# A two-block transformer kernel on one core: convolution taps moved between softmax steps, and VectorE's order at two other places

## The chip, the cores and the metric

One core of a Trainium2 chip. The metric is the device time of one launch in microseconds. Three runs of the kernel before took 1996.96, 1998.6 and 1999.41 us (median 1998.6). The profile shows one more execution of 1994.3 us.

## The reference, cut to what matters

512 tokens of width 1024, fp32, batch 1, two blocks one after the other. Only the parts that the change touches are spelled out.

```python
# first block
x = x + 0.5 * swiglu(rmsnorm(x), ffn1_wgu, ffn1_wdown)
z = rmsnorm(x) @ w_in               # q, k, v | ca, cb | ga, gb
a = sliding_window_attention(q, k, v, sinks) @ attn_proj     # window 128, 16 heads, 2 kv heads
u = ca * sigmoid(cb)
u = causal_depthwise_conv(u, dw_w, dw_b)                     # 31 taps, 1024 channels
c = silu(layernorm(u)) @ conv_proj
x = x + (sigmoid(ga) * a + sigmoid(gb) * c) @ w_out
x = x + 0.5 * swiglu(rmsnorm(x), ffn2_wgu, ffn2_wdown)       # the second FFN
e = rmsnorm(p @ ple_proj)
x = x + sigmoid(rmsnorm(x) @ ple_gate_w) * e
# second block
proj = rmsnorm(x) @ w_in_2          # pool | q, k, v | z | b, a
q, k, v = silu(causal_dwconv(q, k, v, 4 taps))
L = strict_lower(k_beta k^T * decay)                         # chunks of 64, 4 heads
T = inverse(eye + L)                                         # built level by level
# gated delta rule, w_out_2; cross attention to 256 memory tokens; squared-relu FFN of 4096
```

## The kernel before, in words

Activations lie transposed: a tensor of 1024 channels is 8 tiles of 128 channels by 512 tokens. Every large product is done in three matmuls per 128 x 128 x 512 block: with a value split in a high part (fp32r) and the rest as low part, weights high times activations high (L342), high times low (L343), low times high (L346). Weights come in pieces of 128 x 1024 (8 blocks, 24 matmuls: one column of 128 outputs). For each piece SyncE loads `raw`, ScalarE casts it to `whi` (L1093) and VectorE subtracts to get `wlo` (L1768). Three buffers of each go round, so a cast waits until TensorE has done the piece three back.

Each engine's program is written out by hand in its own function, in the order in which the engine runs it; nothing is planned by a program. `weights(upto)` in ScalarE's and VectorE's program casts or subtracts the pieces up to that number, and `after(key)` is `weights(ends[key] + 2)`: two pieces beyond the product named. Engines wait for each other by named events. A product takes one of the 8 banks of PSUM in turn (`take`) and waits until the bank's last user has given it back ("free").

**The softmax stage** has 16 groups of heads and rows. TensorE's step is: a filler product (one column of w_in), the transposes of the probabilities of group i, probabilities times values of group i-1, scores of group i+2. The fillers are ca 4, cb 4, ca 5, cb 5, ca 6, cb 6, ca 7, cb 7, ga 0 to 7, gb 0 and 1; two of them stand ahead of the loop. VectorE's step is `filler` (some taps of the depthwise convolution by `conv(n)`, and for cb the gate in three operations: times_R, the sigmoid by ScalarE, times_R, product with ca into `upad`), the low part of the attention's output, and `soft(i+2)`: maximum, three small operations, two or three taps, then the denominator and its reciprocal. ScalarE's step is the cast of weights, the sigmoid of a cb with a table load ahead of it, copies, and the exponentials (L1278), whose end gives the scores' banks back. The taps (L1884, one scalar_tensor_tensor over 128 x 512 each) are a list of 248, worked off in order in whatever portions `conv(n)` names.

**The second FFN's first weights.** Its pieces are g0, u0, g1, u1, g2 and so on: gate and up columns. Ahead of it stands ple_proj (pl 0 to 7, pieces of 128 x 256), whose result `eb` is squared by ScalarE (`squares`) and summed by VectorE (`add_square`) for the norm of e; the row of means is a matmul behind g1.

**The inverse** in the second block: `products32` is 128 matmuls of 32 x 32 (L691). Level lv is a left product, a mask on VectorE (`left32`, L2305), a right product, and `right32` (L2310: a subtract, then a transpose, L2312). TensorE puts pieces of the z columns (zg 0 to 3) between these products. `chunk(h)` prepares head h, `conv4_in`/`conv4` are the input scaling and four taps of a channel tile, `zgate` scales a z column, and ScalarE's `high(pool_h, ...)` casts the pooled tiles, which lie where the decays of `chunk(3)` lay, so it waits for the last product with them (event `qg`, L2297).

Of the kernel before, what the change touches and what calls it, by code (L numbers as in the profile page):

```python
# [107 lines left out]
def build(nc, io, book, plan):  # L108
# [7 lines left out]
    MUL, ADD, SUB = ALU.mult, ALU.add, ALU.subtract  # L116
    GL, GN = gain_layout()
    ctx = ExitStack()
    with ctx:
# [72 lines left out]
        ph, pl = at("ph", PB + 54272, [128, 2, T], F32R), at("pl", PB + 58368, [128, 2, T], F32R)  # L192
# [90 lines left out]
        def ps(key):  # L283
            return banks[bank_of[key]]
# [797 lines left out]
        def scalar_program(act):  # L1082
# [13 lines left out]
            def after(key):  # L1096
                weights(ends[key] + 2)
# [13 lines left out]
            def squares(name, j, src, n=T):  # L1111

                if j >= 3:
                    act.wait_ge("sum", name, j - 2)
                d = acc[:, 0:n] if j == 0 else scr[3 + j % 2][:, 0:n]
                e.activation(d, src, AF.Square).then_inc(*act.tick("sq", ("sq", name, j)))
# [19 lines left out]
            def norm_row(name, prev, n=T):  # L1136
                b = ps(("R", name))[:, 0:n]
                act.wait_ge("spread", name)
                e.activation(b, b, AF.Ln, bias=epsc, scale=1.0).then_inc(*act.tick("sd", ("ln", name)))
                act.wait_ge("ln", name)  # L1140
                if prev:
                    act.wait_ge("R_done", prev)
                e.activation(Rt[:, 0:n], b, AF.Exp, scale=-0.5).then_inc(*act.tick("R", ("R", name), ("free", ("R", name))))
# [236 lines left out]
            for j in range(8):  # L1380
                after(("pl", j))
            norm_row("f2", "mix")
            for j in range(8):
                act.wait_ge("eb", j)
                if j == 0:
                    act.wait_ge("spread", "f2")
                squares("e", j, eb[:, j, :])

            def glu_e(tag, f):
# [48 lines left out]
            def conv4(i):  # L1438
                s = scr[i % 3][:, :] if i < 8 else vb[:, i - 8, :, :].rearrange("p b c -> p (b c)")
                act.wait_ge("cv_c", i)  # L1440
                e.activation(qkv[:, i, 4:516], s, AF.Silu).then_inc(*act.tick("silu", ("cv", i)))
# [80 lines left out]
            def zgate(i):  # L1522
                act.wait_ge("zg_r", i)
                e.activation(zt[:, i, :], zt[:, i, :], AF.Silu).then_inc(*act.tick("silu", ("z", i)))
# [12 lines left out]
                act.wait_ge("pl", g)  # L1537
                high(pool_h[:, g, :], up[:, g, 16:528], "pool", g)
            after(("cv", 11))
            conv4(11)  # L1540
            zgate(0)
            after(("zg", 0))
            zgate(1)
            after(("zg", 1))
            act.wait_ge("ix5")
# [208 lines left out]
        def vector_program(dve):  # L1754
# [26 lines left out]
            def after(key):  # L1781
                weights(ends[key] + 2)
# [5 lines left out]
            def add_square(name, j, n=T):  # L1788
                dve.wait_ge("sq", name, j)
                if j > 1:  # L1790
                    dve.wait_ge("sum", name, j - 1)
                e.tensor_tensor(acc[:, 0:n], acc[:, 0:n], scr[3 + j % 2][:, 0:n], ADD).then_inc(*dve.tick("sum", ("sum", name, j)))
# [79 lines left out]
            def conv(n):  # L1872

                for j, k in taps[taps_done[0]:taps_done[0] + n]:
                    a = cacc[j % 2][:, :]
                    src, wk = upad[:, j, 2 + k:2 + k + T], gcol("dw_w", 31 * j + k)
                    if k == 0:
                        dve.wait_ge("cb_u", j)
                        if j > 1:
                            dve.wait_ge("conv", j - 2, 30)  # L1880
                        e.tensor_scalar(a, src, wk, gcol("dw_b", j), MUL, ADD).then_inc(*dve.tick("conv", ("conv", j, 0)))
                    else:
                        dve.wait_ge("conv", j, k - 1)
                        e.scalar_tensor_tensor(out=a if k < 30 else upad[:, j, 32:544], in0=src, scalar=wk, in1=a, op0=MUL, op1=ADD).then_inc(  # L1884
                            *dve.tick("conv", ("conv", j, k)))
                    if k == 30 and j:
                        dve.wait_ge("conv", j, 30)
                        if j == 1:
                            dve.wait_ge("cols", "mix")
                            e.tensor_tensor(acc[:, :], upad[:, 0, 32:544], upad[:, 1, 32:544], ADD).then_inc(*dve.tick("sum", ("csum", 1)))  # L1890
                        else:
                            dve.wait_ge("csum", j - 1)
                            e.tensor_tensor(acc[:, :], acc[:, :], upad[:, j, 32:544], ADD).then_inc(
                                *dve.tick("sum", ("csum", j), *([("conv_sum",)] if j == 7 else [])))
                    taps_done[0] += 1
# [74 lines left out]

            def filler(what, j):
                after((what, j))
                conv(5)
                if what == "cb":
                    gate(j)
                elif what == "gb":
                    gate_b(j)
                elif what == "ga":
                    dve.wait_ge("gemm", ("ga", j))
                    times_R(mg[:, j, :], ps(("ga", j))[:, :], "gate", ("ga_r", j), ("free", ("ga", j)))  # L1980
# [134 lines left out]
            for j in range(8):  # L2115
                after(("pl", j))
                dve.wait_ge("gemm", ("pl", j))
                e.tensor_copy(eb[:, j, :], ps(("pl", j))[:, :]).then_inc(*dve.tick("eb", ("eb", j), ("free", ("pl", j))))
            for j in range(1, 8):
                add_square("e", j)  # L2120

            def unit(j):
# [62 lines left out]
            def conv4_in(i):  # L2185
                dve.wait_ge("R", "mix2")
                dve.wait_ge("gemm", ("cv", i))
                times_R(qkv[:, i, 4:516], ps(("cv", i))[:, :], "cv", ("cv_r", i), ("free", ("cv", i)))
# [78 lines left out]
            def first32():  # L2267
                dve.wait_ge("SL", 2)
                dve.wait_ge("SL3")
                dve.wait_ge("cols", ("qk", 3))  # L2270
                e.tensor_tensor(Xs, SL, masks32(0), MUL).then_inc(*dve.tick("held", ("held", 0)))
                dve.wait_ge("held", 0)
                e.tensor_tensor(TTs, id32, Xs, SUB).then_inc(*dve.tick("TT", ("TTs", 0)))
                dve.wait_ge("TTs", 0)
                e.transpose(scr[2][:, :], scr[1][:, :]).then_inc(*dve.tick("TT", ("Tms", 0)))

            def chunk(h):
                dt_, eg, L3, a3 = flat(Xm, h), flat(Tm, h), flat(LT, h), flat(aT, h)
                dve.wait_ge("eg", h)
                e.tensor_copy(eglast[:, 4 * h:4 * h + 4], eg.rearrange("p (c t) -> p c t", t=128)[:, :, 127]).then_inc(*dve.tick("decay", ("el", h)))  # L2280
                dve.wait_ge("kk", h)
                e.tensor_tensor(L3, dt_, ps(("kk", h))[:, :], MUL).then_inc(*dve.tick("chunk", ("L0", h), ("free", ("kk", h))))
                dve.wait_ge("bb", h)
                dve.wait_ge("L0", h)
                e.tensor_tensor(L3, L3, ps(("bb", h))[:, :], MUL).then_inc(*dve.tick("chunk", ("L", h), ("free", ("bb", h))))
                if h == 3:
                    dve.wait_ge("L", h)
                    for a in range(4):
                        s = slice(32 * a, 32 * a + 32)
                        ins = e.tensor_copy(SL[s, 12:16, :], LT[s, 3, :, s])  # L2290
                    ins.then_inc(*dve.tick("SL3", ("SL3",)))
                if h == 3:
                    after(("cv", 10))
                    first32()
                dve.wait_ge("kq", h)
                e.tensor_tensor(a3, dt_, ps(("kq", h))[:, :], MUL).then_inc(*dve.tick("chunk", ("a0", h), ("free", ("kq", h))))
                e.tensor_tensor(qkv[:, h, 4:516], qkv[:, h, 4:516], eg, MUL).then_inc(*dve.tick("chunk", ("qg", h)))  # L2297

            def zgate(i):
                dve.wait_ge("gemm", ("zg", i))  # L2300
                times_R(zt[:, i, :], ps(("zg", i))[:, :], "zg", ("zg_r", i), ("free", ("zg", i)), *([("R_done", "mix2")] if i == 3 else []))

            def left32(lv):
                dve.wait_ge("ix", lv)
                e.tensor_tensor(Xs, blk32(ps(("ix", lv))[:, :]), masks32(lv), MUL).then_inc(*dve.tick("Xm", ("Xs", lv), ("free", ("ix", lv))))  # L2305

            def right32(lv):
                dve.wait_ge("itt", lv)
# [77 lines left out]
                dve.wait_ge("a0", h)  # L2386
                e.tensor_tensor(aT[:, h, :, :], aT[:, h, :, :], inclT.unsqueeze(1).to_broadcast([128, 4, 128]), MUL).then_inc(*dve.tick("aT", ("aT", h)))

            conv4_in(11)
            after(("cv", 11))  # L2390
            left32(1)
            conv4(11)
            right32(1)
            zgate(0)
            after(("zg", 0))
            left32(2)
            pool_low_part(0)
            pool_low_part(1)
            right32(2)
# [371 lines left out]
```

## Time and profile before

| what | value |
|---|---|
| runs, us | 1996.96, 1998.6, 1999.41 |
| profiled execution, us | 1994.3 |
| its span, us | 1992.4 |
| TensorE's granted clock | 0.999 of full speed |
| TensorE busy, us (share) | 1971.0 (99%) |
| VectorE busy, us (share) | 1210.4 (61%) |
| ScalarE busy, us (share) | 824.4 (41%) |
| instructions | 26556 |

Busy times overlap across engines. A row of a timeline gives start, duration, engine, line and operation; what stands in brackets is how long the engine was idle ahead of it and what ended that. Where one row covers several instructions (x5), its duration is of all of them. Durations of following instructions on an engine overlap a little, so the distance of their starts is the better price.

### The profile page before, as it was taken

How to read it: one execution, taken by the hardware profiler on the slowest of the kernel's cores; microseconds unless marked ns; L12 is line 12 of the kernel's file. 1: busy time of each engine (PE TensorE's matmuls, PEld its weight loads, DVE VectorE, ACT ScalarE, POOL GpSimd, SP SyncE). 2: the span in 40 equal slices, each digit the busy share in tenths (PEclk: the TensorE clock that was granted, in tenths of full speed). 3: DMA queues.
4: the chain of work that ended last, by engine and by line, in shares of the span. 5: the costliest groups of instructions: out<-in, count | busy, mean ns of one | idle time of the engine just before them, and what ended most of it. 6: DMA issues, size and time to landing. Idle time of an engine off the chain costs nothing. (4 is left out here: it accounts for less than half of the span.)

```text
span 1992.4 us, 26556 instructions
## 1 busy us (share of the span) xinstructions
PE 1971.0 (99%) x10434; PEld 1616.0 (81%) x10434; DVE 1210.4 (61%) x1708; ACT 824.4 (41%) x1241; POOL 16.2 (1%) x31
## 2 busy tenths in 40 slices
PE   9999999999999999999999999998999999999998
PEld 7888888888677888788888888887988788888887
DVE  6676565688899545654434367886564456544534
ACT  6554343434777353532223255532454442222222
POOL 0000000000000000000000000010000000000000
PEclk9999999999999999999999999999999999999999
DMA  7998897454333552333333233211143323323231
GB/s 253 301 300 291 288 287 254 169 186 165 127 106 127 190 201 85 117 96 100 93 103 96 82 102 95 85 53 30 43 141 113 106 85 96 106 95 96 95 100 69
DMA packets 80922, 275.42 MB, mean 138 GB/s; under 512 B 9216, under 2 KB 11776, under 8 KB 80800
## 3 DMA queue, kind: packets, MB, share of 16 engines
q1 hardware_dynamic: 79648, 272.36, 41.7%
q8 instruction: 83, 1.36, 0.3%
q10 hardware_dynamic: 1152, 1.38, 0.2%
q14 instruction: 39, 0.32, 0.0%
HBM read 240.61 MB, written 32.51 MB: 137 GB/s over the span
## 5 line engine op out<-in xcount | busy, mean ns | idle before, releaser
L342 PE MATMUL ps<-Hh,whi 128*128 128x512 f32 x1456 | 573.1, 394 | 4.2 <-ACT P L1278 2.2
L346 PE MATMUL ps<-Hh,wlo 128*128 128x512 f32 x1456 | 567.3, 390 | 0.5 <-DVE wlo L1768 0.5
L343 PE MATMUL ps<-Hl,whi 128*128 128x512 f32 x1456 | 566.7, 389 | 0.0
L1093 ACT CAST whi<-raw 128x1024 fp32r<-128x1024 f32 (+3 forms) x352 | 350.2, 999 | 383.6 <-PE ps L346 344.9
L1768 DVE TENSOR_TENSOR wlo<-raw,whi 128x1024 fp32r<-128x1024 f32 (+3 forms) x294 | 338.8, 1157 | 181.2 <-ACT whi L1093 174.4
L342 PEld LDWEIGHTS ps<-Hh,whi 128*128 128x128 f32 x1456 | 273.3, 188 | 68.3 <-issue 6.0
L346 PEld LDWEIGHTS ps<-Hh,wlo 128*128 128x128 f32 x1456 | 273.3, 188 | 58.7 <-DVE wlo L1768 1.1
L343 PEld LDWEIGHTS ps<-Hl,whi 128*128 128x128 f32 x1456 | 273.4, 188 | 56.4 <-issue 1.2
L1884 DVE SCALAR_TENSOR_TENSOR cacc<-upad,gains,cacc 128x512 f32<-128x512 f32 x232 | 160.2, 745 | 0.8
L1834 DVE SCALAR_TENSOR_TENSOR x<-ps,x 128x512 f32<-128x512 f32 x79 | 54.6, 691 | 155.1 <-PE ps L346 155.1
L1810 DVE TENSOR_TENSOR scr<-ps,Rt 128x512 f32<-128x512 f32 x92 | 63.2, 687 | 54.8 <-PE ps L346 40.2
L342 PE MATMUL ps<-f3Ah,whi 128*128 128x512 f32 x248 | 96.5, 389 | 0.0
L343 PE MATMUL ps<-f3Al,whi 128*128 128x512 f32 x248 | 96.5, 389 | 0.0
L346 PE MATMUL ps<-f3Ah,wlo 128*128 128x512 f32 x248 | 96.5, 389 | 0.0
L1778 DVE TENSOR_TENSOR lo<-raw,hi 128x1024 fp32r<-128x1024 f32 x58 | 70.9, 1222 | 33.4 <-issue 23.5
L1105 ACT CAST hi<-raw 128x1024 fp32r<-128x1024 f32 x58 | 60.8, 1049 | 46.4 <-DVE lo L1778 27.3
L1109 ACT CAST f3Ah<-scr 128x512 fp32r<-128x512 f32 x32 | 19.9, 621 | 122.7 <-DVE scr L2603 122.7
L342 PE MATMUL ps<-f1Ah,whi 128*128 128x512 f32 x176 | 68.5, 389 | 0.0
L343 PE MATMUL ps<-f1Al,whi 128*128 128x512 f32 x176 | 68.5, 389 | 0.0
L346 PE MATMUL ps<-f1Ah,wlo 128*128 128x512 f32 x176 | 68.5, 389 | 0.0
L342 PE MATMUL ps<-f2Ah,whi 128*128 128x512 f32 x176 | 68.5, 389 | 0.0
L343 PE MATMUL ps<-f2Al,whi 128*128 128x512 f32 x176 | 68.5, 389 | 0.0
(384 smaller groups left out, 2806.2 us busy)
## 6 DMA issues: line engine op xcount, KB each, us to landing
raw<-in_w SPq DMA_DIRECT2D x369, 512.0 KB, 4.0
low_parts<-lo SPq DMA_DIRECT2D x58, 512.0 KB, 4.7
wlo<-low_parts SPq DMA_DIRECT2D x58, 512.0 KB, 3.4
raw<-in_w SPq DMA_DIRECT2D x16, 384.0 KB, 3.1
raw<-in_w SPq DMA_DIRECT2D x17, 256.0 KB, 2.6
out<-y SPq DMA_DIRECT2D x8, 256.0 KB, 2.0
x<-in_x SPq DMA_DIRECT2D x5, 256.0 KB, 6.2
raw<-in_w SPq DMA_DIRECT2D x8, 128.0 KB, 2.0
```

What stands on the lines that cost most here:

```text
L342: e.matmul(out, h[:, kk, :], a, start=part != "last" and k + kk == 0, stop=False)
L343: e.matmul(out, h[:, kk, :], c, start=False, stop=False)
L346: ins = e.matmul(out, lo[:, kk, :], a, start=False, stop=done)
L1093: e.copy(whi[i % WS][:, 0:n], raw[i % RAWS][:, 0:n]).then_inc(*act.tick("whi", ("whi", i)))
L1105: e.copy(hi2[:, :], raw2[m % 2][:, :]).then_inc(*act.tick("hi2", ("hi2", m)))
L1109: e.copy(dst, src).then_inc(*act.tick("hi", ("hi", xn, k), *more))
L1768: e.tensor_tensor(wlo[i % WS][:, 0:n], src, h.bitcast(F32), SUB).then_inc(*dve.tick("wlo", ("wlo", i)))
L1778: e.tensor_tensor(lo2[m % 2][:, :], raw2[m % 2][:, :], hi2[:, :].bitcast(F32), SUB).then_inc(*dve.tick("lo2", ("lo2", m)))
L1810: return e.tensor_tensor(out, src, Rt[:, 0:n], MUL).then_inc(*dve.tick(kind, *names))
L1834: e.scalar_tensor_tensor(out=xj, in0=ps((tag, "d", b, j))[:, :], scalar=scale, in1=xj, op0=MUL, op1=ADD).then_inc(*dve.tick("x", ("x", tag ...
L1884: e.scalar_tensor_tensor(out=a if k < 30 else upad[:, j, 32:544], in0=src, scalar=wk, in1=a, op0=MUL, op1=ADD).then_inc(*dve.tick("conv", ...
```

## The change

Three edits of order. No instruction is added or taken away, and TensorE's list is the same.

1. `filler` on VectorE: eight taps for a ca, two for a cb, in place of five each; other fillers keep five.
2. Second FFN: ScalarE casts g1 ahead of the squares of e and u1 ahead of the sixth square; VectorE subtracts g1 ahead of the second add and u1 ahead of the sixth. Before, both stood behind all squares and adds, in `after(("f2", "u", 0))`.
3. Inverse: on VectorE `conv4_in(11)` moves into `chunk(3)` behind `first32`, level 1's mask `left32(1)` moves from behind the weights of `after(("cv", 11))` to between the two last products of `chunk(3)`, and `conv4(11)` from behind it to behind `left32(2)` and the next weights. ScalarE's `conv4(11)` moves behind `zgate(0)` and those weights.

```diff
@@ ScalarE
             norm_row("f2", "mix")
+            weights(ends["pl", 7] + 3)
             for j in range(8):
                 act.wait_ge("eb", j)
                 if j == 0:
                     act.wait_ge("spread", "f2")
+                if j == 5:
+                    weights(ends["pl", 7] + 4)
                 squares("e", j, eb[:, j, :])
...
             after(("cv", 11))
-            conv4(11)
             zgate(0)
             after(("zg", 0))
+            conv4(11)
             zgate(1)
@@ VectorE
             def filler(what, j):
                 after((what, j))
-                conv(5)
+                conv({"ca": 8, "cb": 2}.get(what, 5))
...
             for j in range(1, 8):
+                if j in (2, 6):
+                    weights(ends["pl", 7] + (3 if j == 2 else 4))
                 add_square("e", j)
...
                     after(("cv", 10))
                     first32()
+                    conv4_in(11)
                 dve.wait_ge("kq", h)
                 e.tensor_tensor(a3, dt_, ps(("kq", h))[:, :], MUL)
+                if h == 3:
+                    left32(1)
                 e.tensor_tensor(qkv[:, h, 4:516], qkv[:, h, 4:516], eg, MUL)
...
-            conv4_in(11)
             after(("cv", 11))
-            left32(1)
-            conv4(11)
             right32(1)
             zgate(0)
+            left32(2)
             after(("zg", 0))
-            left32(2)
+            conv4(11)
             pool_low_part(0)
             pool_low_part(1)
             right32(2)
```

## Rows read from the trace of the kernel before

**Rows 1.** The page's first part: busy us, share of the span, instructions

```profile
PE 1971.0 (99%) x10434; PEld 1616.0 (81%) x10434; DVE 1210.4 (61%) x1708; ACT 824.4 (41%) x1241; POOL 16.2 (1%) x31
```

**Rows 2.** TensorE's waits: us in total, times, longest

```profile
PE ps L691 <- issue: 2.5, 2, 1.3
PE ps L342 <- ACT P L1278: 2.2, 2, 1.5
PE ps L691 <- DVE scr L2305: 2.0, 2, 1.5
...
PE ps L508 <- ACT P L1278: 1.3, 1, 1.3
```

**Rows 3.** TensorE's timeline, softmax stage: start, us, what, idle before

```profile
544.77 0.59 PE L508 MATMUL ps<-maskB,identB 128*128 128x512 bf16 x2 [1.33 <-ACT P L1278]
```

**Rows 4.** VectorE's timeline, softmax stage

```profile
483.93 0.69 DVE L1937 TENSOR_TENSOR scr<-c,scr 128x512 f32<-128x512 f32 x1 [1.40 <-DMA scr<-scr]
...
525.92 3.40 DVE L1884 SCALAR_TENSOR_TENSOR cacc<-upad,gains,cacc 128x512 f32<-128x512 f32 x5
...
530.63 0.69 DVE L1810 TENSOR_TENSOR scr<-scr,Rt 128x512 f32<-128x512 f32 x1 [0.70 <-ACT scr L1211]
```

**Rows 5.** VectorE's scr tiles, 470 to 560: its waits; who waited for it

```profile
  ACT scr L1211: 2.9, 4
...
  ACT scr L1211: 0.5, 2
```

**Rows 6.** ScalarE's timeline, softmax stage

```profile
525.92 1.71 ACT L1287 ACTIVATE P<-P,small 128x256 f32<-128x256 f32 x4 [0.52 <-DVE small L2017]
527.53 1.03 ACT L1093 CAST whi<-raw 128x1024 fp32r<-128x1024 f32 x1
528.58 1.28 ACT L1211 ACT_TABLE_LOAD   x1
529.96 0.63 ACT L1211 ACTIVATE scr<-scr 128x512 f32<-128x512 f32 x1
```

**Rows 7.** TensorE's timeline, second FFN's first columns

```profile
825.38 0.47 PE L342 MATMUL ps<-Hh,whi 128*128 128x512 f32 x1 [1.18 <-ACT whi L1093]
...
826.62 0.50 PE L346 MATMUL ps<-Hh,wlo 128*128 128x512 f32 x1 [0.54 <-DVE wlo L1768]
```

**Rows 8.** VectorE's timeline there

```profile
819.70 5.47 DVE L1792 TENSOR_TENSOR acc<-acc,scr 128x512 f32<-128x512 f32 x7 [3.03 <-ACT scr L1116]
825.33 2.36 DVE L1768 TENSOR_TENSOR wlo<-raw,whi 128x1024 fp32r<-128x1024 f32 x2 [0.17 <-ACT whi L1093]
```

**Rows 9.** ScalarE's timeline there

```profile
818.52 0.62 ACT L1116 ACTIVATE acc<-eb 128x512 f32<-128x512 f32 x1
...
824.20 1.98 ACT L1093 CAST whi<-raw 128x1024 fp32r<-128x1024 f32 x2
```

**Rows 10.** TensorE's timeline, the inverse

```profile
1344.84 1.29 PE L691 MATMUL ps<-scr,scr 32*32 32x32 f32 x128
...
1349.92 1.29 PE L691 MATMUL ps<-scr,scr 32*32 32x32 f32 x128 [1.53 <-DVE scr L2305]
...
1358.12 1.29 PE L691 MATMUL ps<-scr,scr 32*32 32x32 f32 x128 [0.49 <-DVE scr L2305]
```

**Rows 11.** VectorE's timeline, the inverse

```profile
1344.10 0.67 DVE L2297 TENSOR_TENSOR qkv<-qkv,Tm 128x512 f32<-128x512 f32 x1
...
1349.18 0.68 DVE L2305 TENSOR_TENSOR scr<-ps,c 128x512 f32<-128x512 f32 x1
...
1359.46 0.69 DVE L2310 TENSOR_TENSOR scr<-scr,ps 128x512 f32<-128x512 f32 x1 [0.19 <-PE ps L691]
```

**Rows 12.** ScalarE's timeline, the inverse

```profile
1344.81 2.18 ACT L1109 CAST pool_h<-up 128x512 fp32r<-128x512 f32 x4 [3.15 <-DVE qkv L2297]
1346.89 1.04 ACT L1093 CAST whi<-raw 128x1024 fp32r<-128x1024 f32 x1
```

**Rows 13.** DMA queues from 1350 to 1380: packets, MB, share

```profile
q8 instruction: 8, 0.13, 1.8%
```

More of the change, by code:

```diff
@@ L2275, in first32, with left32 @@
                 e.transpose(scr[2][:, :], scr[1][:, :]).then_inc(*dve.tick("TT", ("Tms", 0)))
+            def left32(lv):
+                dve.wait_ge("ix", lv)
+                e.tensor_tensor(Xs, blk32(ps(("ix", lv))[:, :]), masks32(lv), MUL).then_inc(*dve.tick("Xm", ("Xs", lv), ("free", ("ix", lv))))
             def chunk(h):
@@ L2301, in zgate @@
                 times_R(zt[:, i, :], ps(("zg", i))[:, :], "zg", ("zg_r", i), ("free", ("zg", i)), *([("R_done", "mix2")] if i == 3 else []))
-            def left32(lv):
-                dve.wait_ge("ix", lv)
-                e.tensor_tensor(Xs, blk32(ps(("ix", lv))[:, :]), masks32(lv), MUL).then_inc(*dve.tick("Xm", ("Xs", lv), ("free", ("ix", lv))))
             def right32(lv):
```

## The prediction

> **What bounds the kernel now.** I read the page's busy shares first: TensorE is busy 1971.0 us of a span of 1992.4 [rows 1], so all that an order of instructions can win is 21 us of waits, and every microsecond that TensorE is made to wait is paid in full. The view of TensorE's waits says who makes it wait [rows 2]: 3.5 us are banks that ScalarE's exponentials of the softmax give back late (L1278), 2.0 us the inverse's products for a mask by VectorE (L2305), and 2.5 us "issue", waits inside a run of tiny products. The timelines then place them. The change touches three stretches, one for each of its parts; TensorE's own instruction list is not touched.
>
> **Part 1, the taps of the depthwise convolution.** In the softmax stage each of the first eight fillers alternates: "ca" (no gate) and "cb" (with a gate). Before, each has five taps; after, ca has eight and cb two. The number of taps is the same. The question is what decides the length of either kind of step.
>
> Five taps take from 525.92 to 529.25, 0.666 each; so three taps are 2.0 us [rows 4]. In a cb step the gate's second multiply (start 530.63) sat idle 0.70 for ScalarE's sigmoid. The sigmoid waits for the first multiply, but also for ScalarE's own queue: after the reciprocal it scales P (525.92, 1.71), casts weights (527.53, 1.03), loads a table (528.58, 1.28) and only then computes the sigmoid at 529.96, with no idle marked [rows 6]. That queue starts at the reciprocal, not at the taps. So VectorE's taps and ScalarE's queue end together now: with three taps fewer VectorE reaches the gate 2.0 us earlier and waits there; the step gets shorter only by what the sigmoid waited for VectorE. All four gates wait 2.9 us on the sigmoid in sum [rows 5], 0.7 each, which is little more than the sigmoid itself (0.63). The saving is small: two of the four sigmoids, those of cb 4 and 5, waited for VectorE, 0.5 us in sum [rows 5]; I take 0.5, 0.3, 0.1 and 0.1 us for cb 4 to 7. In a ca step nothing of the kind waits: its three extra taps stand ahead of the next maximum, and all that follows (maximum, exponentials, sum, reciprocal, scaling) is 2.0 us later.
>
> One place hides some: before the ninth rope tile VectorE idles 1.40 us for a DMA of turned rows (start 483.93), and ca 4's taps stand ahead of it. The sum, step by step, of VectorE's lateness: ca 4 +2.0 - 1.4 = +0.6; cb 4 takes 0.5 of that back; ca 5 +2.0 and the sum of a finished channel tile (an add of 0.7 to 0.8 us; seven of its kind take 5.47 [rows 8]), which moves ahead of a maximum: +2.7; cb 5 -0.3; ca 6 +2.0; cb 6 -0.1; ca 7 +1.7 (an add moves out); cb 7 -0.1. Together +6.0 us.
>
> Does TensorE have slack against that? No: its last wait of the stage, before L508 at 544.77, is 1.33 us for the exponentials of softmax step 6 [rows 3], the step that follows ca 7. Whatever these are late, the product is late, +6.0, and behind it the ga steps keep their five taps, so nothing is given back. Price of part 1: +6.0 us; its 3.5 us of waits become about 9.5. Bounds: from below -3.5 (these waits vanish, if the gate steps did shorten by 2.0 each); from above +8.0 (four times 2.0, nothing hidden, nothing saved).
>
> The Trainium skill (ScalarE: Activation LUTs, What ACT_TABLE_LOAD costs) gives a switch as 1283 ns and a drain of about 1380 ns, 2.66 us in all. Here the sigmoid starts 1.38 us after the load starts [rows 6]: this trace shows the first figure and no drain. By the page's total ScalarE's queue would be 1.4 us longer in each gate step than in the rows, and VectorE's taps would have had nothing to do with it even before; the sum above uses the row.
>
> **Part 2, the second FFN's first weights.** A column is 24 matmuls, 5.45 us by TensorE's timeline. TensorE reaches the second gate column (piece g1) about 1.2 us before its high part is cast and waits 1.18, then 0.54 for the low part [rows 7]. The cast stands behind eight squares of e, which start at 818.52, and runs only at 824.20, two casts in 1.98 [rows 9]; the low part stands behind seven adds, 819.70 to 825.17 [rows 8]. After, the cast of g1 stands ahead of the squares: 818.5 to 819.5, and everything of that chain moves by 1.0. The first add is at 820.65, then the low part of g1 from 821.3 to 822.5 (one subtract of the 1.14 to 1.2 us kind that runs as a pair in 2.36, just behind the seven adds). TensorE wants it at 824.5 (825.38 less 1.18, and two matmuls): both waits go. The next weights u1: cast in front of the sixth square, about 823.8 to 824.8, low part at 826.0 to 827.2, wanted at 829.9: fine. What is late: the adds end at 828.6 instead of 825.2, and the row of means that reads them stands behind g1, at 829.5 now. The glu of column 0 starts 0.9 later than before while TensorE is 1.9 earlier; its successor weights g2 have their low part by 834.3 and are wanted at 835.4. So no new wait, with 1 us to spare. Gain: 1.18 + 0.54 = 1.72, plus the restart of the pipeline lost at each, about 0.15: -1.9. Bounds: -2.1 and 0 (if the 1 us is used up, g2 is late by as much).
>
> **Part 3, the inverse's levels.** The product of level 1's right side waits 1.53 for the mask (L2305), level 2's 0.49 [rows 10]. The mask runs at 1349.18 although its input, the product that starts at 1344.84 and takes 1.29, is there at 1346.1 [rows 10]: it stands behind a low part of weights whose cast ScalarE does at 1346.89, behind four casts that take 1344.81 to 1346.89 and wait for the last product with eg (L2297, 1344.10) [rows 11, 12]. After, the mask stands ahead of that, at 1346.2 to 1346.9, so the product can start at 1348.4: -1.5. But L2297 is now behind the mask: it ends at 1347.5, ScalarE's four casts run until 1349.6, the weights of z1 are cast by 1350.6 and their low part is there at 1352.0. TensorE wants it at 1351.5: a new wait of 0.5. VectorE stands at that low part too, so level 1's second half ends at 1353.3 (0.6 earlier than before) and TensorE's left product of level 2 starts at 1353.4: gain so far 0.7. Then the left mask of level 2 is no longer behind z2's weights, its 0.49 goes, and the right product starts at 1356.9: 1.2 gained. The convolution of tile 11 (four operations like a tap [rows 4], about 2.8) now stands ahead of level 2's end: VectorE reaches that (L2310, 1359.46 before) at 1360.7 and ends at 1362.2, and TensorE wants it at 1362.3: just in time.
>
> Last, the "issue" waits. The trace has 8 instruction blocks fetched in 30 us here [rows 13], one in about 3.7 us, against 83 in the whole span. TensorE's 128 tiny products and as many weight loads pass in 1.3 us [rows 10], so that in this stretch it runs into the end of what is fetched; the two waits of 2.5 us [rows 2] lie in products with no large matmul ahead. These blocks are called for as TensorE moves on, so they come earlier when it does. I take -1.5 for part 3; bounds -1.9 (all of 2.02 less a restart) and 0 (the fetches take it back, or the weights of z1 are later).
>
> The Trainium skill (Runtime: NRT & Kernel Launch, Instruction fetch mechanics) says blocks of 16 KiB, 256 instructions, are fetched in order and that this is mostly hidden. No run so far shows these waits to be the fetch; if they are, it is not hidden here.
>
> **Sum.** +6.0 - 1.9 - 1.5 = +2.6 us. The profiled execution took 1994.3 (span 1992.4), below the three timed runs, whose median is 1998.6; by it the changed kernel would profile at 1996.9. On the median: 2001.2 us.
>
> **Rivals.**
> A. The gate steps do get shorter (the other side). If ScalarE's queue were not the limit, VectorE's steps would be even, 2.0 less in each cb step against 2.0 more in each ca step, and the 3.5 us of bank waits would go: 1998.6 - 3.5 - 1.9 - 1.5 = 1991.7. It decides if the sigmoid, in the changed kernel, starts within 1 us of the first multiply. For it: the gate's work (three operations) is on VectorE and that engine has no other idle time there. Against it: the sigmoid starts right behind the table load in the row.
> B. Only half of the lateness reaches TensorE: banks run ahead by a step, say +3: 1998.6 + 3.0 - 3.4 = 1998.2. For it: TensorE starts the stage with no wait up to 524.8. Against: it ends with one.
> C. Part 1 as forecast but parts 2 and 3 give nothing, each turned into a later wait (weights g2; weights of z1 and the fetch): 1998.6 + 6.0 = 2004.6.
>
> **How the numbers follow.** Forecast 0.56 (1999.5 to 2003.5 with its bounds and the scatter of the runs, 2.5 us), B 0.20, C 0.10, A 0.14. Range: 1995.0 to 2004.5; left out are A and a tail of C. 0.2% is 4.0 us, about what a measurement of this kernel tells from no change: faster means under 1994.6, slower over 2002.6. Faster: A and a tail of B, 0.16. Slower: most of C and a third of the forecast, 0.27. Same: 0.57.
>
> **What would show it.** Right: TensorE's waits on ScalarE's P (L1278) grow from 3.5 to about 9; VectorE's idle time before the gate's second multiply grows from 2.9 to about 10; no wait of TensorE behind the first columns of the second FFN; first wait on L2305 gone, and a wait for weights of about 0.5 in its place. Wrong: those waits on P shrink (A); waits in the second FFN turn up at g2; "issue" grows by what L2305 loses.

## The result: 2002.2 us, 4 us slower; right in sign and nearly in size

Thirteen runs of the changed kernel have a median of 2002.15 us (1999.32 to 2006.79), thirteen of the kernel before beside them 1999.06 (1995.07 to 2002.15): ratio 1.0021 [1.0011, 1.003], so +4.2 us [2.2, 6.0], where +2.6 was forecast. By the forecast's own classes (slower only over 2002.6 us) the median counts as "same", which it had as the likeliest. The profiled execution took 2005.92 us (span 2004.1) at a mean granted clock of 0.992, the lowest of its thirteen (the others 0.994 to 0.998; before 0.999). The two profiled executions are thus 11.6 us apart where the medians are 3.1: that of after shows more lost to the clock than most runs had, that of before nearly nothing; so a second profile of the same kernel is read beside it below.

The page's first part, and TensorE's waits (line waited for: us in total, times, longest), both of after. The change shifts line numbers: L2305 of before is L2284 now, L2297 is L2309, L2310 is L2318, L1768 is L1771:

```profile
PE 1982.2 (99%) x10434; PEld 1624.2 (81%) x10434; DVE 1210.2 (60%) x1708; ACT 823.8 (41%) x1241; POOL 16.2 (1%) x31
```

```profile
PE ps L342 <- ACT P L1278: 4.0, 2, 2.5
PE ps L366 <- issue: 3.1, 1, 3.1
PE ps L508 <- ACT P L1278: 3.1, 1, 3.1
PE ps L691 <- issue: 2.0, 2, 1.3
...
PE ps L368 <- DVE wlo L1771: 0.2, 1, 0.2
```

Beside [rows 2]: the waits on P went from 3.5 to 7.1, both waits for the mask are gone, and one wait for instructions inside the inverse (L366) has grown from 1.1 to 3.1. But TensorE is also *busy* 11.2 us longer than in [rows 1] with the same 10434 matmuls. That is the clock: each window below has its PEclk, and half of the 23.8 us in which it was low is 11.9 (it is low again at the end of either span, once TensorE has no more to do). Windows of after (us: PE busy, PEld, DVE, ACT, POOL, then PEclk, DMA share, GB/s):

```profile
509.00:517.00 8.00, 6.99 (x18) 5.52 (x19) 4.83 (x11) 7.44 (x18) 0.00 (x0) 0.57 0.08 31
550.00:558.00 8.00, 6.85 (x21) 4.46 (x22) 4.18 (x9) 7.44 (x17) 0.00 (x0) 0.57 0.03 8
1297.00:1302.00 5.00, 5.00 (x19) 4.07 (x20) 4.83 (x9) 1.45 (x2) 0.00 (x0) 0.66 0.21 83
1369.00:1377.00 8.00, 6.79 (x144) 5.58 (x144) 2.77 (x5) 1.56 (x2) 0.00 (x0) 0.57 0.01 2
```

In each the granted clock is at the lower of its two levels, 1.2 GHz instead of 2.4, for part of the window: 6.8, 6.8, 3.4 and 6.8 us (narrower windows put the start of the low clock at 509.3, 550.3, 1297.6 and 1369.5). The softmax stage shows what came before (TensorE's timeline, after):

```profile
510.01 0.79 PE L342 MATMUL ps<-Hh,whi 128*128 128x512 f32 x1 [2.51 <-ACT P L1278]
510.60 0.63 PE L343 MATMUL ps<-Hl,whi 128*128 128x512 f32 x1
...
551.15 1.01 PE L508 MATMUL ps<-maskB,identB 128*128 128x512 bf16 x2 [3.10 <-ACT P L1278]
```

L508 stood at 544.77 [rows 3] and is now 6.4 later. The matmul behind 510.01 lasts 0.63 instead of 0.39 (the same line at 504.89), and the 1.2 GHz stretch behind 551.15 makes 6.4 us of lateness into 9.1 (matched matmul by matmul up to the second FFN). The first such stretch cost nothing at the end of the stage: the next wait on P took it up.

### The profile page after: what moved, and what is told of

Same layout as the page of the kernel before. It is cut to its first block, busy times and chain, and to the rows that moved or that the text cites. A ratio compares the mean times of both kernels' runs of the same rounds, so it can differ in the third digit from the quotient of the medians.

```text
span 2004.1 us, 26555 instructions
## 1 busy us (share of the span) xinstructions
PE 1982.2 (99%) x10434; PEld 1624.2 (81%) x10434; DVE 1210.2 (60%) x1708; ACT 823.8 (41%) x1241; POOL 16.2 (1%) x31
## 4 chain that ended last, share of the span: by engine, by line
PE 94%; DVE 3%; ACT 2%; issue 1%; DMA 0%; ACTq 0%; POOL 0%; POOLq 0%; DVEq 0%
PE ps L342 27%; PE ps L346 27%; PE ps L343 27%; DVE cacc L1887 1%; PE ps L365 1%; PE ps L366 1%; PE ps L368 1%; PE ps L921 1%; PE ps L904 1%; ACT P L1278 1%; PE ps L376 1%; PE ps L534 1%; PE ps L384 1%; PE ps L512 1%; PE ps L691 0%
## 5 line engine op out<-in xcount | busy, mean ns | idle before, releaser
L1771 DVE TENSOR_TENSOR wlo<-raw,whi 128x1024 fp32r<-128x1024 f32 (+3 forms) x294 | 338.8, 1157 | 177.3 <-ACT whi L1093 170.8
```

The source lines that it names most:

```text
L1771: e.tensor_tensor(wlo[i % WS][:, 0:n], src, h.bitcast(F32), SUB).then_inc(*dve.tick("wlo", ("wlo", i)))
```

## Part 1: what a gate step waits for

VectorE (first fence) and ScalarE (second) in a gate step of after: start, us, what, idle before and for whom:

```profile
531.81 0.68 DVE L1813 TENSOR_TENSOR scr<-ps,Rt 128x512 f32<-128x512 f32 x1
535.25 0.69 DVE L1813 TENSOR_TENSOR scr<-scr,Rt 128x512 f32<-128x512 f32 x1 [2.76 <-ACT scr L1211]
```

```profile
530.62 1.71 ACT L1287 ACTIVATE P<-P,small 128x256 f32<-128x256 f32 x4 [0.51 <-DVE small L2020]
532.24 1.03 ACT L1093 CAST whi<-raw 128x1024 fp32r<-128x1024 f32 x1
533.29 1.28 ACT L1211 ACT_TABLE_LOAD   x1
534.58 0.64 ACT L1211 ACTIVATE scr<-scr 128x512 f32<-128x512 f32 x1
```

ScalarE's queue is that of [rows 6] shifted whole: from the scaling to the sigmoid 3.96 us, before 4.04. The sigmoid starts 2.77 us behind the start of the first multiply, so rival A, which needed less than 1, is out. Over the four gates VectorE's idle time rose from 2.9 us [rows 5] to that of this row (VectorE's scr tiles, 470 to 566):

```profile
  ACT scr L1211: 10.2, 4
```

**Part 1 alone** (e_taps, four runs).

```diff
-                conv(5)
+                conv({"ca": 8, "cb": 2}.get(what, 5))
```

> Part 1 alone. My theory: the ca steps get 2.0 us longer each and the gate steps do not get shorter, because ScalarE's queue (scale, cast, table load, sigmoid) ends the gate. Waits of TensorE on ScalarE's P (L1278) of 7 us as in the changed kernel (4.0 + 3.1), L508 of softmax group 7 starts at about 551.1 (544.8 before), VectorE idle before the gate's second multiply about 10 us in sum (2.9 before). On top, the granted clock: if a long wait makes it fall, it is at half from 509 to 516 and from 550 to 557 again, and the columns behind are 9 us late, not 6. Time: +6 to +9 us. Rival (the clock's falls are chance and have nothing to do with the waits): +6 us, and they stand elsewhere or nowhere.

2005.98 us, 1.0044 [1.0027, 1.0061]: +8.8 us [5.4, 12.2]. L508 stands at 551.23, 6.5 later; gate waits 10.2; waits on P 5.1 and 3.1. The clock fell at 511.4, 552.3 and 1368.1. So part 1 is the whole loss. Whether it is larger than the 6.0 of the forecast four runs don't tell: 6 lies within the interval.

```profile
551.23 0.59 PE L508 MATMUL ps<-maskB,identB 128*128 128x512 bf16 x2 [3.10 <-ACT P L1278]
```

**Part 1 with the sigmoid ahead of the cast** (e_taps_sig): if ScalarE's queue ends the gate, taking the 1.03 us cast out of it must give back about that per gate.

```diff
             def filler(what, j):
+                if what == "cb":
+                    sigmoid_gate(j)
                 after((what, j))
-                if what == "cb":
-                    sigmoid_gate(j)
```

> Part 1, and ScalarE does the sigmoid of a gate ahead of the cast of weights instead of behind it. Theory (ScalarE's queue ends the gate step): each gate step gets shorter by the cast, 0.95 us; VectorE's idle time before the second multiply falls from about 2.5 to about 1.5 per gate; L508 of group 7 starts 2.1 us earlier than with the taps alone, at about 549. Time -2 us against the taps alone, +4 against before. Rival (VectorE's taps set the step): no change against the taps alone.

2004.6 us, 1.003 [1.0019, 1.0042]: +6.0 us against before, where +4 was expected, and 2.8 below part 1 alone, where 2 was. Gate waits 6.4 instead of 10.2, 0.95 less per gate, and L508 at 548.94, 2.3 earlier: ScalarE's queue is what the gates wait for. The stage's end kept its wait of 3.1 and the clock fell behind it again (548.7), and also behind a wait on P of 1.7 (528.1):

```profile
527.89 0.56 PE L342 MATMUL ps<-Hh,whi 128*128 128x512 f32 x1 [1.70 <-ACT P L1278]
...
548.94 1.01 PE L508 MATMUL ps<-maskB,identB 128*128 128x512 bf16 x2 [3.09 <-ACT P L1278]
```

**Only the gates eased, in the kernel before** (e_gate): the same swap of ScalarE's, and cb steps with one tap ahead and three inside the gate, in the shadow of the sigmoid. The tap count of the gate steps is 4 instead of 5: the work is the same, four taps of it run later.

```diff
-                conv(2 if 1 <= j < 4 else 0)
+                conv(2 if 1 <= j < 4 else 3 if j > 3 else 0)
...
-                conv(5)
+                conv({"cb": 1}.get(what, 5))
```

> The kernel before, with the softmax's gate steps eased where my theory says they are bound: ScalarE does the sigmoid ahead of the cast of weights, and VectorE does one tap ahead of the gate and three between its first multiply and its second, in place of five ahead (four taps fewer in all, which are done behind the stage). Theory: each gate step gets about 1 us shorter, VectorE's idle time before the second multiply is 0, L508 of group 7 starts 3 us earlier than before (541.9), waits on P (L1278) fall from 3.5 to 2.0 us. Time -3 us. Rival (the step is bound by something else): TensorE starts that product at 544 or later, time the same.

1995.46 us, 0.9987 [0.9978, 0.9997]: -2.6 us. L508 at 542.42, gate waits 1.2 in two gates, waits on P 1.5. The swap alone could not have done this, by the rows of before: the sigmoid starts at 529.96 [rows 6], and the first multiply, which it needs, ends only at 529.93; cast and taps have to move together. VectorE, before:

```profile
529.25 0.68 DVE L1810 TENSOR_TENSOR scr<-ps,Rt 128x512 f32<-128x512 f32 x1
```

Of the 2.5 us by which TensorE is ahead behind the stage 1.2 went again where the convolution's sum is read: the four taps that run later arrive late there (e_best below, where none is late, has no such wait). TensorE, e_gate:

```profile
661.80 1.12 PE L392 MATMUL ps<-acc,cg 128*128 128x512 f32 x2 [1.02 <-DVE acc L1893]
```

**Part 1 undone in the changed kernel** (e_undo1: parts 2 and 3).

```diff
-                conv({"ca": 8, "cb": 2}.get(what, 5))
+                conv(5)
```

> The changed kernel with part 1 undone (five taps each). Theory: waits on P as before (3.5 us), no fall of the clock in the softmax stage, the second FFN's waits gone (-2.2); in the inverse -1.5 to +1 without the clock. Time -1 to -3.5 us against before, and 6 to 9 us below the changed kernel. Rival (the parts work on each other, the inverse loses 3 us as in the changed kernel's profile each time): +1 us.

1994.52 us, 0.9987 [0.9978, 0.9996], so -2.6 us, as expected. Gate waits 2.9 again, waits on P 2.3 and 1.3, no fall of the clock in the stage. Against the changed kernel's +4.2, part 1 inside the whole change is thus worth about 6.8 us, less than the 8.8 it gave alone. Its issue wait is still 1.9, so the longer issue wait does not need part 1.

**The changed kernel once more** (e_after_again), for a second profile.

> The changed kernel itself once more, for a second profile beside the first. Softmax stage: the same waits within 0.2 us and the clock at half twice, behind the waits of 2.7 and 3.5 us. Inverse: issue wait 1.8 to 1.9 us if its block's fetch comes ahead of the weight load, about 3.1 if behind; both are possible. The fall of the clock near 1298 us, where TensorE waits for nothing, may be there or not.

2002.63 us, 1.0028 [1.0016, 1.004]. The waits came as expected, the two falls of the clock in the softmax stage did not. Its waits, and the two windows in which the first profile had half the clock:

```profile
PE ps L342 <- ACT P L1278: 5.7, 3, 2.5
PE ps L508 <- ACT P L1278: 3.1, 1, 3.1
...
PE ps L366 <- issue: 2.3, 1, 2.3
```

```profile
509.00:517.00 8.00, 6.92 (x34) 5.23 (x34) 4.82 (x11) 7.44 (x19) 0.00 (x0) 1.00 0.11 34
550.00:558.00 8.00, 6.76 (x33) 5.06 (x34) 4.17 (x9) 7.45 (x18) 0.00 (x0) 1.00 0.03 12
```

Behind the same waits of 2.5 and 3.1 us the clock stays at 1.00, and L508 stands at 551.24: 6.5 us is what part 1 costs in waits, whatever the clock does. Here waits on P come to 8.8, against a forecast of 9.5 from 3.5.

How often the clock falls, the runs' mean granted clock tells: 0.9958 over the 31 runs of the four kernels with steps of eight and two taps and the old order of ScalarE (changed kernel, e_after_late, e_after_again, e_taps), 0.9970 over 76 runs of the kernel before, 0.9974 over 79 runs of the eight kernels without such steps. What a clock lower by 0.0012 costs is an estimate: 2.4 us if all of 2000 us went with it; a line through the times against the clocks has a slope of 1.2 us for each 0.001 in the first group, 1.6 in the second and 0.8 in the third, which makes it 1.0 to 1.9. With 6.5 of waits that is 7.5 to 8.9 for part 1. The times don't settle it: they give 8.8 for the part alone and about 6.8 inside the change.

The Trainium skill (TensorE: Matmul & The Clock Gate, Part 1: The HAM clock gate) says the clock is set by how busy the engine has been, and names idling as what lowers it. The traces agree in part: falls followed waits of 2.5 and 3.1 us, but the second profile shows the same waits with no fall, and the fall at 1297 in after has no wait ahead of it. That fall is not at a random place, though: ahead of it TensorE does 2.8 us of tiny products (1294.7 to 1297.5), and in seven of the fourteen profiles the clock falls at this same place of the program.

```profile
1296.61 1.05 PE L376 MATMUL ps<-cg,scr 128*128 128x1 f32 x8
1297.53 0.58 PE L342 MATMUL ps<-Hh,whi 128*128 128x512 f32 x1
```

## Part 2 alone

**e_ffn**: the second FFN's order only, ScalarE's and VectorE's lines of the diff under `weights(ends["pl", 7] + 3)` and `+ 4`.

> Part 2 alone. Theory: the two waits of 1.18 and 0.54 us at the second FFN's g1 go and nothing comes in their place: -2.2 us up to the third gate column, time -2 us. Rival: a wait at g2 gives it back: 0.

1994.87 us, 0.9985 [0.9976, 0.9995]: -3.0 us [-4.8, -1.0]; in its profile TensorE gains 2.3 across g1 (the two waits and the restarts), as in after, where its lateness goes from 9.05 to 6.8. A wait of 0.3 for an earlier low part, which after does not have, took 0.5 of it in e_ffn. The order came out as worked out, seen in after: the forecast's times plus 9.1, by which the stretch is late. ScalarE's casts of g1 and u1 (forecast 818.5 and 823.8):

```profile
827.54 1.04 ACT L1093 CAST whi<-raw 128x1024 fp32r<-128x1024 f32 x1
...
832.72 1.03 ACT L1093 CAST whi<-raw 128x1024 fp32r<-128x1024 f32 x1
```

VectorE's first add (820.65), low parts (821.3, 826.0) and last adds (end 828.6):

```profile
829.66 0.69 DVE L1795 TENSOR_TENSOR acc<-acc,scr 128x512 f32<-128x512 f32 x1 [3.97 <-ACT scr L1116]
830.27 1.22 DVE L1771 TENSOR_TENSOR wlo<-raw,whi 128x1024 fp32r<-128x1024 f32 x1
...
834.93 1.22 DVE L1771 TENSOR_TENSOR wlo<-raw,whi 128x1024 fp32r<-128x1024 f32 x1
836.06 1.48 DVE L1795 TENSOR_TENSOR acc<-acc,scr 128x512 f32<-128x512 f32 x2
```

## Part 3 alone, and the wait for instructions

**e_inv**: the inverse's order only (`left32(1)` behind the last head, the weights and `conv4(11)` behind `left32(2)`).

> Part 3 alone. Theory: the right product of level 1 starts 1.5 us earlier, but the issue wait behind the right product of level 2 grows from 1.1 to about 3.1 us, because the instruction blocks are fetched late: 3.0 us late in the chain of blocks, since two of their fetches queue behind weight loads of 256 KB that now fall just ahead of them. Sum over the inverse 0 to +0.5 without the clock; if the clock falls behind the 3.1 us wait as in the changed kernel, +2.7 more. Time +0.5 to +3 us. Rival (the long issue wait of the changed kernel was chance): the wait is about 1.1 as before, time -1.5 us.

1997.1 us, 0.9993 [0.9984, 1.0002]: -1.4 us, not told from none. The wait at L366 is 1.8 us, not the 3.1 expected, and the time is not the +0.5 to +3 expected: the long wait of after is not this part's alone. TensorE, the inverse in after:

```profile
1353.25 1.29 PE L691 MATMUL ps<-scr,scr 32*32 32x32 f32 x128
...
1356.74 1.48 PE L691 MATMUL ps<-scr,scr 32*32 32x32 f32 x128
...
1360.41 0.50 PE L368 MATMUL ps<-Hh,wlo 128*128 128x512 f32 x1 [0.16 <-DVE wlo L1771]
...
1361.76 1.29 PE L691 MATMUL ps<-scr,scr 32*32 32x32 f32 x128
...
1365.24 1.42 PE L691 MATMUL ps<-scr,scr 32*32 32x32 f32 x128
1366.59 0.50 PE L365 MATMUL ps<-Hh,whi 128*128 128x512 f32 x1
1370.21 0.79 PE L366 MATMUL ps<-Hl,whi 128*128 128x512 f32 x1 [3.12 <-issue]
```

Set against [rows 10] the first product is 8.4 late, the next 6.8 (1.6 won, forecast 1.5), the third 7.7 (0.7, forecast 0.7), the fourth 7.1 (1.3, forecast 1.2), and then the matmul behind it 9.3: all is lost in one wait for instructions. That wait was there before, too, and the prediction, which read only the two inside the tiny products (L691), passed it over. In before:

```profile
1360.93 0.50 PE L366 MATMUL ps<-Hl,whi 128*128 128x512 f32 x1 [1.08 <-issue]
```

The DMA view shows that wait's cause (after, 1364 to 1372, forty slices of 0.2 us: busy tenths, GB/s):

```profile
DMA  0000000000089644440300000000000000000040
GB/s 0 0 0 0 0 0 0 0 0 0 0 143 246 184 184 184 174 164 20 92 0 0 0 0 0 0 0 0 0 0 0 0 0 0 0 0 0 0 82 0
...
q8 instruction: 2, 0.03, 1.7%
```

A load of 256 KB of weights fills the DMA engines from 1366.2 to 1367.6; right behind it, at 1367.8, comes one instruction block, and TensorE goes on at 1370.2, 2.4 us later. No line of the kernel places the blocks, but one places the load.

**Loads held until level 4's left product is done** (e_after_late on the changed kernel, e_inv_late on part 3 alone, e_late on the kernel before).

```diff
+            weights(ends["zg", 3])
+            sp.wait_ge("ix", 4)
             weights(ends["w2", 7] + 2)
```

> The kernel before with the same two loads held, no part of the change. Theory: fetches 3.5 to 3.9 us apart and none later than 8.9 us after the first right product; issue wait 1.1 us in this and not 2.2 or 2.6 as in two kernels that have this stretch unchanged. Time the same as before within 1 us. Rival: the wait scatters up to 2.6 us here too.

> Part 3, and SyncE holds the two weight loads of 256 KB that fall in the inverse (w_pool_2 and the first of w_out_2) until the left product of level 4 is done. Theory (blocks of instructions queue behind weight loads): the fetch that starts late (9.4 to 11.2 us after the first right product in the kernels with part 3) starts at about 8.7, the issue wait behind the right product of level 2 is 1.3 us or less (3.1 in the changed kernel, 1.8 with part 3 alone), the clock does not fall in the inverse, and the last matmul is 1.0 to 1.5 us earlier than before. Rival (the fetch is late by itself, whatever else the queues do): issue wait 1.8 to 3.1 as with part 3 alone.

> The changed kernel with the two weight loads of the inverse held until the left product of level 4 is done. Theory: the 3.1 us of issue wait in the changed kernel are about 1.9 of waiting for a block of instructions that is asked for only when TensorE comes near, plus 1.3 that its fetch stood behind a weight load; with the load held: issue wait 1.6 to 1.9 us, fetch at 9.4 to 9.5 us after the first right product (11.15 in the changed kernel). Rival (scatter of the fetch itself): 3 us again. Waits on P and the clock's falls in the softmax stage as in the changed kernel.

With the hold, e_after_late has no load in this place (1362 to 1372, slices of 0.25 us); the block comes at 1366.4 (the slice from 1366.25), 1.2 behind the start of the fourth product, and the wait is 1.76:

```profile
DMA  0030000000000000020000000000000030000000
GB/s 0 0 66 0 0 0 0 0 0 0 0 0 0 0 0 0 0 66 0 0 0 0 0 0 0 0 0 0 0 0 0 0 66 0 0 0 0 0 0 0
```

```profile
1365.21 1.42 PE L691 MATMUL ps<-scr,scr 32*32 32x32 f32 x128
...
1368.82 0.50 PE L366 MATMUL ps<-Hl,whi 128*128 128x512 f32 x1 [1.76 <-issue]
```

Narrow windows of the DMA view give the start of the blocks in all profiles; four of them, in us:

| profile | third product | block | fourth product | next block | TensorE goes on | wait |
|---|---|---|---|---|---|---|
| before | 1354.08 | 1355.1 | 1358.12 | 1358.7 | 1360.93 | 1.1 |
| e_after_late | 1361.73 | 1362.7 | 1365.21 | 1366.4 | 1368.82 | 1.8 |
| after | 1361.76 | 1362.8 | 1365.24 | 1367.9 | 1370.21 | 3.1 |
| e_ffn | 1355.91 | 1355.3 | 1359.39 | 1359.1 | 1361.36 | 0.3 |

One block comes 0.9 to 1.1 us behind the start of the third product in eleven of the fourteen profiles, so it does follow TensorE. The next, which the matmul behind the fourth product needs, comes 3.3 to 3.9 us behind that block, or 4.1 to 5.1 where a load stands in front of it, and TensorE goes on 2.3 to 2.7 us after it starts. The fourth product stood 4.04 behind the third in before and stands 3.48 behind it now: the 0.5 us won there turns into waiting, because the block does not come sooner.

The L366 waits of all profiles: with the inverse unchanged 1.1 (before), 1.1 (e_late), 1.3 (e_gate), 2.2 (e_taps), 2.6 (e_taps_sig), and 0.3 in e_ffn and e_best2, where the clock was low for 3.4 us ahead of the third product, so that TensorE came later and the blocks did not; with part 3, 1.8 (e_inv), 1.6 (e_inv_late), 1.9 (e_undo1), 1.8 (e_after_late), 1.5 (e_best), 2.3 and 3.1 (changed kernel). So, those two aside, two things add up. The order of part 3 makes it 0.2 to 0.8 longer, load or no load; and a load in front of the block adds 0.4 to 1.6. That is one profile of each kernel, two of the changed one. The block starts where the load ends in e_taps, e_taps_sig and both profiles of the changed kernel, the four longest. e_inv_late missed what was expected of it: its wait is 1.6 and not 1.3 or less, its block comes 9.4 behind the first right product and not 8.7, and the clock fell in its inverse (1363). The waits of e_late and e_after_late came as expected. In time the hold is worth nothing that can be told: e_late 1997.14 us, 0.9997 [0.9988, 1.0006]; e_inv_late 1996.27, 0.9992 [0.9983, 1.0002]; e_after_late 2002.67, 1.002 [1.0011, 1.003], as the changed kernel.

## A version that beats both

Parts 2 and 3, the sigmoid ahead of the cast, and five taps in every step: two ahead of a gate and three inside it, so that none is late (e_best); the same without part 3 (e_best2). Against the changed kernel, besides the swap in e_taps_sig:

```diff
-                conv(2 if 1 <= j < 4 else 0)
+                conv(2 if 1 <= j < 4 else 3 if j > 3 else 0)
...
-                conv({"ca": 8, "cb": 2}.get(what, 5))
+                conv({"cb": 2}.get(what, 5))
```

> Parts 2 and 3 of the change with the gate steps eased: ScalarE's sigmoid ahead of its cast of weights, and of the five taps of a gate step two ahead of the gate and three between its first multiply and its second, so that no tap is left for later. Theory: the stage 2.5 us shorter than before (gate waits 0), nothing given back at the row of means of the convolution (1.1 us with four taps fewer), no wait above 2 us and so no fall of the clock in the stage; -2.2 us in the second FFN; the inverse 0 to -1.5. Time -5 to -6 us against before, about 1992. Rival: the stage is still paced by VectorE, -2.5 us in all.

> The same without part 3: the inverse as before. Theory: -4.5 us against before; e_best is 0 to 1.5 us below it, which is what part 3 is worth. Rival (part 3 only adds issue waits): this is as fast as e_best or faster.

e_best: 1993.36 us, 0.9976 [0.9966, 0.9986], -4.8 us (-5 to -6 was expected). e_best2: 1993.33, 0.9978 [0.9969, 0.9987], -4.4 us. Both beat the kernel before and, by the ratios to it, the changed one by some 9 us. TensorE's waits of e_best on P and in the inverse, and the end of its softmax stage:

```profile
PE ps L366 <- issue: 1.5, 1, 1.5
...
PE ps L508 <- ACT P L1278: 1.3, 1, 1.3
...
PE ps L342 <- ACT P L1278: 0.7, 1, 0.7
```

```profile
542.48 0.59 PE L508 MATMUL ps<-maskB,identB 128*128 128x512 bf16 x2 [1.34 <-ACT P L1278]
```

The two do not differ, so part 3 is worth nothing that this measurement can show.

## Why the prediction held, step by step

The parts run alone add up: +8.8 - 3.0 - 1.4 = +4.4, the change +4.2. The sum is better than its terms: parts 2 and 3 together give 2.6 (e_undo1), not 4.4, which leaves about 6.8 for part 1; each of these has an interval of 2 to 3 us to either side. Against the forecast's terms the errors are of either sign, a dearer part 1 and, alone, a better part 2, so that a total 1.6 us off is in part luck.

- **Part 1, forecast +6.0.** The mechanism was right: gate steps end with ScalarE's queue, the three taps taken out of them save nothing, the three put into the other steps cost 2.0 each. L508 came 6.4 later in the profile of after, 6.5 in e_taps and the second profile; idle time at the gates 10.2 against "about 10"; waits on P 7.1, 8.2 (e_taps) and 8.8 against 9.5 (in the profile with 7.1 the slow clock filled part of them). The term left something out: it priced a wait of TensorE as its length only, and the lower clock behind such waits, an estimated 1.0 to 2.4 us, is missing.
- **Part 2, forecast -1.9.** Right in mechanism, a little small: 2.3 won across g1 in the profiles of e_ffn and after, because the restarts cost 0.56 and not 0.15; -3.0 [-4.8, -1.0] timed. g2's weights came in time, as worked out with 1 us to spare.
- **Part 3, forecast -1.5.** The products moved as forecast; a wait for the weights of z1 was there in four of seven profiles, 0.16 to 0.36 instead of 0.5. The step that failed is "These blocks are called for as TensorE moves on, so they come earlier when it does". It holds for the block behind the third product's start and not for the next, which follows that one by 3.3 us or more (1362.7 and 1366.4 in e_after_late), and TensorE goes on some 2.4 us later. The mask wait of 0.49 in [rows 10] had hidden part of that; when it went, the issue wait took its place, and a load in front took the rest in the profile of after. Where no load stands in front, the profiles with part 3 keep 0.5 to 0.8 us of the won time past this wait; the two of the changed kernel lose 0.3 and 0.9. Timed alone the part gave -1.4 [-3.2, +0.4], within the change nothing visible. How much of it a typical run keeps stays open.
- **Rivals.** A fell with the 2.77 us of the sigmoid. B (half of the lateness) is refuted by L508. C (2004.6) is further from the median of 2002.15 than the forecast (2001.2), and part 2 did give its gain; of its two reasons only the one on the fetch is seen. What the forecast called wrong, "issue" growing by what L2305 loses, did mostly happen in the profile of after: 2.0 lost there, 2.0 more at L366, 0.5 less at L691.

## What to carry over

A step shared by two engines ends with the longer queue: taking work from the other gives nothing, and what is put elsewhere is paid in full, so put filler work *inside* the wait, not in front of it or into the next step. Before a wait is priced as removed, look for the next one it was hiding, instruction fetches included. In a kernel that is 99% busy on TensorE a wait of some microseconds can cost more than its length (6.4 us late became 9.1 in after). Whether spreading the same waiting thinly would be worth something by itself no run here tests.

## What the runs showed of the hardware

- The granted clock falls to half for 3.4 or 6.8 us at a time in a kernel that keeps TensorE 99% busy, between none (before) and four times (after, e_after_late, e_taps_sig) in a profile while products run; each fall costs up to 2.7 us. It differs between executions of one kernel, but the places recur: the inverse in eleven of the fourteen profiles, right behind 2.8 us of tiny products (1294.7 in after) in seven. In the softmax stage it fell in four of the five profiles with waits of 3.1 us there, and in none of the nine without. The mean clock goes with 54% of the scatter (variance) of the 76 runs of the kernel before and 57% of the 31 with those waits, but with only 10% of the 79 others.
- A run of 128 products of 32 by 32 in 1.3 us lets TensorE run out of instructions for 0.3 to 3.1 us: it goes on 2.3 to 2.7 us after the needed block starts, which comes 3.3 us or more after the block before, and a 256 KB load ahead of the block on the DMA engines makes it longer. The Trainium skill (Runtime: NRT & Kernel Launch, Instruction fetch mechanics) says such fetches are mostly hidden; for these products the trace disagrees, with 5.1 us of issue waits in after.
